# Two transformer blocks in one kernel: the three mixers of block 1 are interleaved with the groups of its input projection, which keep two PSUM banks

## The reference

```python
u = h @ w_in[i]                                  # 1024 -> 352 + 1536 + 768 columns
u_mla, u_diff, u_sb = jnp.split(u, [MLA_IN, MLA_IN + DIFF_IN], axis=-1)
y_mla  = mla_mixer(u_mla, ...)    # latents -> rms_norm -> q, k, v of 4 heads, rope, softmax, times v
y_diff = diff_mixer(u_diff, ...)  # 4 heads: softmax(q1 k1 + bias) - lam * softmax(q2 k2 + bias), times v, rms_norm
y_sb   = sb_mixer(u_sb)           # 4 heads: stick-breaking weights from softplus and a reversed cumulative sum
mix = jnp.concatenate([y_mla, y_diff, y_sb], axis=-1) @ w_o[i]
h = layer_norm(DEEPNORM_ALPHA * h + mix, ...)
ffn = grouped_moe(h, ...)         # 16 experts, 2 per token
ple = jax.nn.sigmoid(h @ ple_gate[i]) * (p[i] @ ple_proj[i])
h = layer_norm(DEEPNORM_ALPHA * h + ffn + ple, ...)
```

## Time and profile before

| what | value |
|---|---|
| median of 3 runs | 1936.86 us (1933.1 to 1937.24) |
| profiled execution, own time | 1930.9 us |
| its span in the profile | 1929.1 us |
| mean granted clock of TensorE | 0.935 |
| busy share PE, DVE, ACT | 88%, 44%, 27% |

### The profile page before, as it was taken

One profiled execution on the slowest core, in us unless ns is written; L12 is line 12 of the kernel. 1 busy time (PEld: TensorE's weight loads), 2 busy tenths in 40 slices (PEclk: granted clock), 3 DMA queues, 4 the chain that ended last, 5 costly groups with the idle time before them and its releaser, 6 DMA issues.

```text
span 1929.1 us, 23107 instructions
## 1 busy us (share of the span) xinstructions
PE 1702.4 (88%) x9305; PEld 1210.2 (63%) x9307; DVE 843.6 (44%) x1774; ACT 517.1 (27%) x934; POOL 0.5 (0%) x7
## 2 busy tenths in 40 slices
PE   7958999999895899999879986586889999899998
PEld 6646444444564744444347555586789995479998
DVE  7885410000404541000044455655555663746655
ACT  1144111010214311111032351121244442355443
POOL 0000000000000000000000000000000000000000
PEclk9959999999996899999999868697999999999999
DMA  9062489999606158999962000000434443303541
GB/s 312 1 240 61 167 332 392 396 392 363 239 1 240 40 181 327 392 397 392 365 239 87 1 1 1 1 1 1 162 145 175 174 174 131 131 1 124 183 174 65
DMA packets 153356, 347.06 MB, mean 180 GB/s; under 512 B 8240, under 2 KB 15280, under 8 KB 153280
## 3 DMA queue, kind: packets, MB, share of 16 engines
q1 hardware_dynamic: 145904, 338.28, 47.5%
q10 hardware_dynamic: 7376, 7.74, 1.3%
HBM read 344.96 MB, written 1.05 MB: 179 GB/s over the span
## 4 chain that ended last, share of the span: by engine, by line
PE 74%; DMA 10%; DVE 9%; ACT 3%; issue 2%; SPq 2%; DVEq 0%; ACTq 0%
PE ps L749 70%; DMA ring<-in_w_up 8%; DVE ring L1914 3%; SPq L655 2%; DVE arena L1914 1%; DMA ring<-in_w_ff 1%; PE ps L1146 1%; DVE ring L1920 1%; DMA ring<-in_w_in 1%; PE ps L756 1%; DVE ring_r L1914 0%; DVE small L2082 0%; ACT arena L1445 0%; DVE ring L1917 0%; PE ps L842 0%
## 5 line engine op out<-in xcount | busy, mean ns | idle before, releaser
L749 PE MATMUL ps<-ring,arena 128*64 128x512 f32 (+6 forms) x1728 | 388.5, 585 | 28.1 <-DMA ring<-in_w_up 17.6
L749 PE MATMUL ps<-arena_r,ring_r 128*128 128x272 f32 (+1 forms) x1152 | 328.1, 285 | 0.0
L749 PEld LDWEIGHTS ps<-ring,arena 128*64 128x64 f32 (+2 forms) x1728 | 141.9, 146 | 257.1 <-issue 250.0
L1445 ACT ACTIVATE arena<-ps 128x512 f32<-128x512 f32 (+7 forms) x179 | 79.8, 475 | 536.0 <-PE ps L749 327.1
L749 PEld LDWEIGHTS ps<-arena_r,ring_r 128*128 128x128 f32 x1152 | 217.3, 189 | 0.0
L749 PE MATMUL ps<-arena_r,ff_hi_r 128*128 128x272 f32 (+1 forms) x1056 | 205.4, 286 | 2.8 <-DVE hT L1914 2.8
L749 PE MATMUL ps<-arena_r,y_r 128*128 128x272 f32 (+1 forms) x592 | 164.0, 288 | 10.3 <-DVE h_r L1914 4.8
L749 PEld LDWEIGHTS ps<-arena_r,ff_hi_r 128*128 128x128 f32 x1056 | 166.9, 189 | 3.6 <-DVE hT L1914 3.2
L749 PE MATMUL ps<-ring 128*128 128x128 f32 (+2 forms) x848 | 132.6, 324 | 38.0 <-DVE ring L1914 30.6
L749 PE MATMUL ps<-arena 128*128 128x512 f32 (+8 forms) x418 | 123.5, 497 | 36.4 <-DVE small L1917 18.0
L749 PE MATMUL ps<-h_r,y_r 128*128 128x272 f32 (+1 forms) x528 | 151.1, 286 | 0.0
(11 more groups left out here) (298 smaller groups left out, 2039.3 us busy)
## 6 DMA issues: line engine op xcount, KB each, us to landing
ring<-in_w_down SPq DMA_DIRECT2D x32, 2048.0 KB, 14.5
ring<-in_w_gate SPq DMA_DIRECT2D x32, 2048.0 KB, 17.4
ring<-in_w_up SPq DMA_DIRECT2D x32, 2048.0 KB, 19.2
ring<-in_w_ff SPq DMA_DIRECT2D x32, 2048.0 KB, 8.7
ring<-in_w_in SPq DMA_DIRECT2D x8, 2048.0 KB, 19.3
ring<-in_w_in_ab SPq DMA_DIRECT2D x5, 2048.0 KB, 12.8
ring<-in_w_o SPq DMA_DIRECT2D x4, 2048.0 KB, 11.2
ring<-in_ple_gate SPq DMA_DIRECT2D x4, 2048.0 KB, 19.4
```

Source lines behind the costliest of these rows:

```text
L749: return pe.matmul(o, lhsT, rhs, start=a, stop=z)
L1445: return act.activation(o, i, ACT.Copy, scale=scale)
```

## The change

The 18 groups are cut into pieces, and the stages of the mixers stand between the pieces, on PE and with the copies on ACT. The groups rotate over banks 6 and 7 alone, so that banks 0 to 5 are the mixers'; a group waits for the copy of the group two before it, where it was four before. The blocks for the stick-breaking queries and keys (slot 4) are loaded and projected before the differential values (slot 3). In the first layer the stick-breaking mixer stands ahead of the differential one, whose bias DVE builds in smaller pieces until then; in the second the differential mixer runs between the latent one and the stick-breaking one. The turned probabilities get buffers of their own (before, they lay in `hT`, which the projection still reads), and so do the latent probabilities and the stick-breaking arrays. ACT loads the table set for exponential and logarithm once, ahead of the copies of the projection (`log_exp_table`); before, three table loads stood among the exponentials of each layer. The number of matmuls, copies and elementwise operations is the same.

The functions that are not shown here (`expand_latents`, `turn_heads`, `latent_scores`, `diff_scores`, `stick_scores`; on ACT and DVE likewise) hold the statements that stood there before, with other banks.

```diff
-        pT = hT_t[:, 0:1024].rearrange("p (b h q) -> p b h q", b=2, h=4)
-        zm = view(4608, SB_H * 384, pat="p (h w) -> p h w", h=SB_H)
-        zt = view(6144, SB_H * 384, pat="p (h w) -> p h w", h=SB_H)
+        pT = [view(6144, 512, pat="p (b h q) -> p b h q", b=1, h=4), view(6656, 1024, pat="p (b h q) -> p b h q", b=2, h=4)]
+        zm = view(8768, SB_H * 384, pat="p (h w) -> p h w", h=SB_H)
+        zt = view(4608, SB_H * 384, pat="p (h w) -> p h w", h=SB_H)
...
         U_GROUPS = [(0, None, t, MLA_IN) for t in range(NT)] \
             + [(1, j, None, P) for j in range(4)] + [(2, j, None, P) for j in range(4)] \
-            + [(3, None, t, 512) for t in range(NT)] + [(4, j, None, P) for j in range(4)] \
+            + [(4, j, None, P) for j in range(4)] + [(3, None, t, 512) for t in range(NT)] \
             + [(5, None, t, SB_W) for t in range(NT)]
         NU = len(U_GROUPS)
+        MLA_T_BANK = [(3,), (4, 5)]
+        MLA_O_BANK = [3, 2]
+        DIFF_S_BANK = [[(4, 5), (2, 0)], [(0, 1), (0, 4)]]
+        DIFF_T_BANK = [[(4,), (0, 1)], [(4,), (5, 4)]]
+        DIFF_O_BANK = [[5, 2], [4, 5]]
+        SB_O_BANK = [[6, 7], [0, 1]]
...
             for l in range(DEPTH):
-                for i, (c0, n) in enumerate(W_COLS):
+                for i in (0, 1, 2, 4, 3, 5):
+                    c0, n = W_COLS[i]
...
-                for i, (s, j, t, n) in enumerate(U_GROUPS):
-                    if l > 0 and i == 1:
...
-                    if i >= 4:
-                        pe.wait_ge(u_ev, NU * l + i - 3)
-                    b = 4 + i % 4
...
+                def project(first, end):
+                    for i in range(first, end):
+                        s, j, t, n = U_GROUPS[i]
+                        if l > 0 and i == 1:
+                            normed_tile(2 * l - 1, 1)
+                            normed_tile_in(2 * l - 1, 1)
+                        if i == 0 or U_GROUPS[i - 1][0] != s:
+                            pe.wait_ge(slot_full[s], full(l, s))
+                        if i >= 2:
+                            pe.wait_ge(u_ev, NU * l + i - 1)
+                        b = 6 + i % 2
...
+                def turn_latents():
+                    pe.wait_ge(mla_norm, l + 1)
+                    for t in range(NT):
+                        pe.transpose(ps[:, 0, t * P:(t + 1) * P], cqn[:, t, 0:P], ident)
+                        pe.transpose(ps[0:MLA_QR - P, 0, S + t * P:S + (t + 1) * P], cqn[:, t, P:MLA_QR], ident)
+                        ins = pe.transpose(ps[:, 1, t * P:(t + 1) * P], ckn[:, t, :], ident)
+                    ins.then_inc(cT_mm, 1)
...
+                def turn_probs(t, src, banks):
                     for b in range(t + 1):
                         for hd in range(4):
-                            ins = pe.transpose(ps[:, 6 + b, hd * P:(hd + 1) * P], src[:, hd, b * P:(b + 1) * P], ident)
+                            ins = pe.transpose(ps[:, banks[b], hd * P:(hd + 1) * P], src[:, hd, b * P:(b + 1) * P], ident)
                     ins.then_inc(pT_mm, 1)
-                    pe.wait_ge(pT_ev, n + 1)
+                def weigh(t, v, dvw, out_bank):
                     for hd in range(4):
                         for b in range(t + 1):
-                            ins = mm(ps[:, out_bank, hd * dvw:(hd + 1) * dvw], pT[:, b, hd, :], v(b, hd), b == 0, b == t)
+                            ins = mm(ps[:, out_bank, hd * dvw:(hd + 1) * dvw], pT[t][:, b, hd, :], v(b, hd), b == 0, b == t)
                     ins.then_inc(o_mm, 1)
+                def latent_turn():
+                    for t in range(NT):
+                        pe.wait_ge(s_exp, 4 * l + t + 1)
+                        turn_probs(t, m_prob[t], MLA_T_BANK[t])
+                def latent_weigh():
+                    for t in range(NT):
+                        pe.wait_ge(pT_ev, 4 * l + t + 1)
+                        weigh(t, lambda b, hd: mv[:, b, hd, :], MLA_V, MLA_O_BANK[t])
...
+                def diff_turn(t):
                     pe.wait_ge(p_ready, 2 * l + t + 1)
-                    pe.wait_ge(o_ev, 4 * l + t + 1)
-                    probs_times_v(4 * l + 2 + t, t, prob[0][t], lambda b, hd: dv[:, b, hd * DIFF_V:(hd + 1) * DIFF_V], DIFF_V, 4 + t)
+                def diff_weigh(t):
+                    weigh(t, lambda b, hd: dv[:, b, hd * DIFF_V:(hd + 1) * DIFF_V], DIFF_V, DIFF_O_BANK[l][t])
...
+                def stick_sums():
+                    pe.wait_ge(z_sp, l + 1)
...
+                def stick_weigh():
+                    pe.wait_ge(u_ev, NU * (l + 1))
+                    pe.wait_ge(z_exp, l + 1)
...
+                project(0, 5)
+                turn_latents()
+                project(5, 6)
+                expand_latents()
+                project(6, 8)
+                turn_heads()
+                project(8, 9)
+                latent_scores()
+                project(9, 11)
+                latent_turn()
+                if l > 0:
+                    pe.wait_ge(u_ev, NU * l + U_LAST[2])
+                    pe.wait_ge(s_ready, 4 * l + 2)
+                    diff_scores(0)
+                project(11, 12)
+                if l > 0:
+                    pe.wait_ge(s_ready, 4 * l + 3)
+                    pe.wait_ge(pT_ev, 4 * l + 2)
+                    diff_scores(1)
+                latent_weigh()
+                project(12, 15)
+                pe.wait_ge(o_ev, 4 * l + 2)
+                if l > 0:
+                    pe.wait_ge(s_ready, 4 * l + 4)
+                pe.wait_ge(u_ev, NU * l + U_LAST[4])
+                stick_scores()
+                project(15, 16)
+                if l > 0:
+                    diff_turn(0)
+                    stick_sums()
+                    pe.wait_ge(pT_ev, 4 * l + 3)
+                    diff_turn(1)
+                    project(16, 17)
+                    pe.wait_ge(pT_ev, 4 * l + 4)
+                    diff_weigh(0)
+                    diff_weigh(1)
+                    project(17, 18)
+                    stick_weigh()
+                else:
+                    stick_sums()
+                    project(16, 17)
+                    diff_scores(0)
+                    project(17, 18)
+                    pe.wait_ge(z_arg, l + 1)
+                    diff_scores(1)
+                    stick_weigh()
+                    for t in range(NT):
+                        diff_turn(t)
+                        pe.wait_ge(pT_ev, 4 * l + 3 + t)
+                        diff_weigh(t)
...
+                log_exp_table()
+                def evict(first, end):
+                    for i in range(first, end):
+                        s, j, t, n = U_GROUPS[i]
+                        act.wait_ge(u_mm, NU * l + i + 1)
...
+                evict(0, 5)
+                latents_out()
+                evict(5, 6)
+                act.wait_ge(lam_ready, l + 1)
+                act.activation(lam_e, lam, ACT.Exp).then_inc(lam_exp, 1)
+                keys_values_out()
+                evict(6, 8)
+                heads_out()
+                evict(8, 9)
+                latent_exps(0)
+                evict(9, 10)
+                latent_exps(1)
+                evict(10, 11)
                 for t in range(NT):
-                    prob_T(4 * l + 2 + t, t)
-                act.wait_ge(z_arg, l + 1)
-                act.activation(zm[:, :, :], zm[:, :, :], ACT.Exp).then_inc(z_exp, 1)
-                for t in range(NT):
-                    act.wait_ge(sbo_mm, 2 * l + t + 1)
-                    copy(y[:, t, DM - SB_W:DM], ps[:, t, 0:SB_W]).then_inc(sbo_ev, 1)
+                    prob_T(4 * l + t, t, MLA_T_BANK[t])
+                if l > 0:
+                    diff_exps(0)
+                    evict(11, 13)
+                    diff_exps(1)
+                    evict(13, 15)
+                    softplus()
+                    evict(15, 16)
+                    for t in range(NT):
+                        prob_T(4 * l + 2 + t, t, DIFF_T_BANK[l][t])
+                    stick_exp()
+                    evict(16, 18)
+                    stick_out()
+                else:
+                    evict(11, 15)
+                    softplus()
+                    evict(15, 16)
+                    stick_exp()
+                    evict(16, 18)
+                    diff_exps(0)
+                    stick_out()
+                    diff_exps(1)
+                    for t in range(NT):
+                        prob_T(4 * l + 2 + t, t, DIFF_T_BANK[l][t])
...
-                    edges(4, 23)
+                    edges(4, 7)
...
-                    edges(23, 25)
+                    edges(7, 11)
...
+                def latent_out():
+                    for t in range(NT):
+                        dve.wait_ge(o_mm, 4 * l + t + 1)
...
+                if l == 0:
+                    latent_out()
+                    edges(18, 23)
+                    stick_masked()
+                    edges(23, 25)
+                    stick_softplus()
+                    edges(25, 27)
```

(20 more changed lines are left out.)

278 lines of the change are left out of this document (133 added, 145 removed).

## The result

| | before | after |
|---|---|---|
| median | 1934.98 us (4 runs, 1932.93 to 1937.24) | 1878.71 us (4 runs, 1875.59 to 1883.7) |
| ratio of the two | | 0.972, 95% interval 0.970 to 0.9741 |
| profiled execution, own time | 1930.9 us | 1878.13 us |
| its span | 1929.1 us | 1876.3 us |
| granted clock, mean | 0.935 | 0.95 |

The changed kernel is faster by 2.6 to 3.0% (95% interval). The predicted 1884 lies 5.3 us above the measured median, and inside the predicted range, 1875 to 1901. The difference of the two profiled executions, 1930.9 less 1878.13, is 52.8 us, which is also what the prediction's sum came to.

What follows compares the result with a forecast made beforehand. No engine was full in the old serial mixers; interleaved, PE would bound the second layer and DVE the first. Gains of 38.0 and 14.8 sum to 52.8 us, and 1936.9 - 52.8 = 1884 us, range 1875 to 1901.

Steps and rivals of the forecast that it cites:

- the new wait: Second layer, before the first query group: PE waits 2.65 us for the first latent group's copy, behind the table load.
- the early latent pieces: Second layer: the latent mixer's early PE pieces, at 2.4 GHz already, cost 11.01 us.
- the pieces that stood between 588.3 and 630.9: Second-layer mixers: 21.63 us busy at mean clock 0.56 become 12.1 at full clock; other bound, no gain.
- the other waits: Second layer: PE waits about 0.6 us at the softplus chain and 0.8 at the last copies; 1.4 in the sum.
- The second mask: First layer, differential mixer: if DVE never waits, this mask is ready at 125.5, where it ended at 131.39.
- The half clock of the tail: End of the first layer's stage: transposes and products at the lower clock; at full clock they would take 3.0 us less.
- The rival of the weight stream: Expert loads not starting earlier: the first layer's 14.8 us lost, 1899, or no change, 1937; chance 0.04.
- Partial overlap: Both stages: late copies or masks stop PE, or small pieces gain no clock; gain 15 to 45 us; chance 0.17.
- The falling clock: Projection groups of both layers: TensorE drops to 1.2 GHz and stays, time near 2040; chance 0.03.
- the drain: Skill rule for the second layer's table load: about 1.38 us added per switch, wait 4.0, time 1.4 us longer.
- the swing of the clock with cycled banks: Skill rule for the projection groups: small idles while cycling PSUM banks swing the clock; two banks step that way.
- the median of the runs is 6.0 above it: Whole kernel: the earlier median, 1936.9, taken as 6.0 us above the profiled 1930.9, so 1878.1 becomes 1884.

Runs made afterwards that it cites:

- l1_apart: The changed kernel with the interleaving undone in the second layer alone, its 18 groups first on the same two banks: 1915.97 us.
- l0_27_steps: The changed kernel with 27 of the 30 bias steps, the last three edges left out of the table: 1876.2 us.
- l0_diff_first: The changed kernel with the first layer in the second layer's order, differential mixer ahead of the stick-breaking one: 1895.62 us.
- before_table: The kernel before with only the table set for exponential and logarithm loaded once ahead of the projection's copies: 1928.03 us, one execution.
- l0_tail_busy: The changed kernel with constant matmuls, five and six, in two PE waits at the end of the first layer's stage: 1882.83 us.
- the three `l1_apart` kernels: `l1_apart` (1915.97 us) and two versions of it with added constant matmuls in PE's second-layer mixer waits, differently placed: 1919.78 and 1917.01 us.

## Why the prediction was right

**Second layer, 38.0 forecast, 39.3 measured.** Term by term, from 498.49, by PE's starts in the trace of after: the 16 groups 62.8 (forecast 62.2); the new wait 2.65 (2.65); the early latent pieces 10.1 (11.0); the pieces that stood between 588.3 and 630.9 now 11.0, in place of 21.63 (12.1); sums and what stands by them 5.4 (5.8); the last product 2.9 (2.7); the other waits 1.7 (1.4). The sum is 96.5, forecast 97.9. That overlap is the cause is shown by `l1_apart`, which loses 37.4 us. That the pieces gain the full clock was the term with the widest bounds, 12.1 to 21.63; it came out at 11.0, below the lower one. A busy time multiplied by the mean clock of its whole stretch, idle time with it, is an estimate, and here it was 1.1 too high.

**First layer, 14.8 forecast, 14.4 measured.** The second mask was ready at 125.51 (forecast 125.5), the turning of `y` began at 147.82 (147.4). The half clock of the tail was as forecast, and the tail took 22.3 us (forecast 21.9). The 125.5 is exact by luck in part: the prediction had the triangle sums ready 1.2 us before DVE wants them, and DVE waited 0.62 for them (108.88), because they began at half clock; against that it began the fifth bias step 0.35 earlier (39.49 for 39.84) and had 0.3 less work. That DVE is the bound holds by a small margin alone, as `l0_27_steps` shows: the prediction did not say how close PE is behind it. That the overlap is the cause in this layer is read from the timeline and from `l0_diff_first` and `l0_27_steps`; no run undoes it there.

**Transfers.** The first expert load moved by 14.4 us in the first layer. In the second it was issued at 669.32 before and is at 616.50 now, 52.8 earlier. The rival of the weight stream falls for this change.

**The other rivals.** Partial overlap: of the places where a late copy or mask could stop PE in the second layer, two did before its last wait for `y`, for 0.70 and 0.47. The falling clock: 1.00 over the second layer's stage, 0.97 over the first's up to 125.5, where the triangle sums alone began at half clock. Both weighed rules would have made the time longer: the drain (4.0 for the wait; it was 2.65), and the swing of the clock with cycled banks (Trainium skill, TensorE: Matmul & The Clock Gate, A second HAM failure mode), which neither the changed kernel nor `l1_apart` shows, whose bare groups ran at 1.00 from 503.5 on.

**The term that was off** is the last one, "the median of the runs is 6.0 above it". The profiled execution of after lies 0.6 under its median, and the median of before came out at 1932 to 1935 later on, where three runs had given 1936.86. On the profiled executions the sum was exact to 0.1 us, by luck in part: 1.3 too little for the second layer and 0.8 behind it were offset by 0.4 too much for the first, 0.1 among the experts and the 1.6 of a slower first group.

## What to carry to other kernels

When a serial chain between engines follows a stage in which one engine is full, cost the interleaving as the full engine's work at full clock, and then check the other engines for one that has a load of its own: that one is the new bound, and how close the next is behind it should be stated too. Order the chains so that the one which needs the loaded engine's result comes last; with the order of the second layer the first layer gave nothing. Don't pay for clock alone: fillers in a chain that stays serial gave 3 us of the 13 that PE's pieces lost at half clock in the kernel before, because only a few of its pieces are on the path and the clock fell again behind the next wait that was left open. When a control run differs from the old kernel by almost nothing, look whether two effects cancel in it: here 4.9 us gained in the chain and 4.4 lost with two banks.

## What the hardware showed that I had not expected

Shortening a wait can cost what it saves: in `before_table` 1.28 us less of waiting was followed by products at half clock, 3.78 for 2.05. And the same wait can cost more or less. In two profiles of the changed kernel the wait of 2.65 us was followed by three groups in 10.60 us. In `l0_27_steps`, whose second layer is the same code, it was not:

```profile
497.47 12.29 PE L757 MATMUL ps<-hT,ring 128*128 128x256 f32 x48 [2.65 <-ACT arena L1524]
```

Over all the profiles here, the groups began at half clock behind this wait in six of eight (`l0_diff_first`, `l0_tail_busy` and the three `l1_apart` kernels are the others), and the two that did not are those of the changed kernel, in which the first latent group had taken 8.03 or 8.04 us, in all others 6.39 to 7.60. Where the early table load had cut the wait to 1.38 or 1.37, in three profiles, they ran at full clock each time (10.60). That the shorter wait protects the clock is therefore likely, but three profiles do not show it. Each of these places was worth up to 1.8 us either way in kernels with the same code there; what decides is not shown. What lies behind the second layer's turning of `y` took between 1277.9 and 1286.9 us in the kernels profiled here, none of which changes it, and that hides anything under some 4 us in a total time.
